# A two-layer hybrid attention block: one software pipeline per layer over the passes of all three branches

## What is computed

```
h = rmsnorm(x) * (1 + scale) + shift        # scale, shift, gate from silu(c) @ ada_w
mla:  q, k, v through low ranks (384, 256), part of q and k rotated; keys: 256 context + 512 image
swa:  8 query, 2 key heads; keys: 256 context + a band of 128 each side; a sink in the softmax
ax:   8 query, 2 key heads, q and k normalised per head and rotated; all 768 keys
y_b = (softmax(q k^T) v * silu(z_b)) @ w_o_b               for b in mla, swa, ax
x   = x + gate * ((sum_b sigmoid(g_b) * y_b) @ w_out)
```

## Time and profile before

| | |
|---|---|
| median of three runs | 2379.16 us |
| the profiled execution | 2383.12 us, span 2383.2 us |
| TensorE busy, weight loads | 1965.2 us (82%), 1676.0 us (70%) |
| VectorE, ScalarE, GpSimd busy | 1079.5 us (45%), 893.4 us (37%), 622.4 us (26%) |
| chain of work that ended last | TensorE 61%, VectorE 20%, ScalarE 8%, GpSimd 5%, issue 4%, DMA 2% |
| projections in that chain | L941, 48% |
| data moved | 125.90 MB, mean 53 GB/s |

### The profile page before, as it was taken

One profiled execution on the slowest core, in us unless ns is written; L12 is line 12 of the kernel. 1 busy time (PEld: TensorE's weight loads), 2 busy tenths in 40 slices (PEclk: granted clock), 3 DMA queues, 4 the chain that ended last, 5 costly groups with the idle time before them and its releaser, 6 DMA issues.

```text
span 2383.2 us, 27657 instructions
## 1 busy us (share of the span) xinstructions
PE 1965.2 (82%) x11005; PEld 1676.0 (70%) x11005; DVE 1079.5 (45%) x2189; ACT 893.4 (37%) x1631; POOL 622.4 (26%) x328
## 2 busy tenths in 40 slices
PE   4487777998888997787998967777997889676987
PEld 2376666888777885676887956666786778566767
DVE  0334667202566215787322343666224652568323
ACT  2323445312445213665322122444322442456332
POOL 5411110223100232222343231120342015220452
PEclk7597999999879997998998977898997799789999
DMA  5200000222000221122223110000231013200342
GB/s 191 69 24 19 18 18 1 53 71 71 18 5 10 53 76 47 42 62 54 75 84 125 47 63 24 14 23 14 80 98 36 5 28 102 62 14 1 84 133 98
DMA packets 183441, 125.90 MB, mean 53 GB/s; under 512 B 6478, under 2 KB 178064, under 8 KB 183312
## 3 DMA queue, kind: packets, MB, share of 16 engines
q1 hardware_dynamic: 177520, 108.57, 16.3%
q10 hardware_dynamic: 5792, 15.56, 1.9%
HBM read 119.91 MB, written 4.19 MB: 52 GB/s over the span
## 4 chain that ended last, share of the span: by engine, by line
PE 61%; DVE 20%; ACT 8%; POOL 5%; issue 4%; DMA 2%; ACTq 0%; DVEq 0%; SPq 0%
PE acc L941 48%; PE wide L964 4%; PE ptp L979 3%; DVE nmax L1477 3%; DVE pt_m L1495 2%; PE acc L999 2%; DVE e_m L1490 2%; POOL swapped L1308 2%; POOL rot L1311 2%; ACT pt_m L1202 2%; PE acc L1000 2%; DVE o_t L1502 1%; ACT e_m L1193 1%; DVE swapped L1381 1%; DVE rot L1382 1%
## 5 line engine op out<-in xcount | busy, mean ns | idle before, releaser
L1287 POOL TENSOR_TENSOR w_lo<-w_raw,w_hi 128x1024 fp32r<-128x1024 f32 (+3 forms) x236 | 494.9, 2109 | 1366.7 <-ACT w_hi L1126 1366.6
L941 PE MATMUL acc<-h_hi,w_hi 128*128 128x512 f32 (+2 forms) x1288 | 470.9, 366 | 27.6 <-POOL h_lo L1320 14.7
L941 PE MATMUL acc<-h_lo,w_hi 128*128 128x512 f32 (+2 forms) x1288 | 468.9, 364 | 0.0
L941 PE MATMUL acc<-h_hi,w_lo 128*128 128x512 f32 (+2 forms) x1288 | 468.3, 364 | 0.0
L941 PEld LDWEIGHTS acc<-h_hi,w_hi 128*128 128x128 f32 (+1 forms) x1288 | 252.0, 196 | 70.3 <-POOL h_lo L1320 15.5
L1126 ACT ACTIVATE w_hi<-w_raw 128x1024 fp32r<-128x1024 f32 (+3 forms) x236 | 216.4, 932 | 195.3 <-PE acc L941 146.1
L941 PEld LDWEIGHTS acc<-h_hi,w_lo 128*128 128x128 f32 (+1 forms) x1288 | 251.2, 195 | 36.6
L941 PEld LDWEIGHTS acc<-h_lo,w_hi 128*128 128x128 f32 (+1 forms) x1288 | 251.2, 195 | 35.9
L1477 DVE TENSOR_REDUCE nmax<-wide 128x1 f32<-128x768 f32 (+4 forms) x240 | 189.4, 789 | 22.1 <-PE wide L964 11.0
L1495 DVE TENSOR_TENSOR pt_m<-ptp,pt_m 128x512 fp32r<-128x512 f32 x208 | 142.4, 687 | 96.4 <-ACT pt_m L1202 95.1
L1160 ACT ACTIVATE th<-acc 128x512 f32<-128x512 f32 x108 | 56.9, 527 | 338.1 <-PE acc L941 336.9
(11 more groups left out here) (183 smaller groups left out, 3717.4 us busy)
## 6 DMA issues: line engine op xcount, KB each, us to landing
w_raw<-in_w_in SPq DMA_DIRECT2D x102, 512.0 KB, 3.9
w_raw<-in_ada_w SPq DMA_DIRECT2D x48, 512.0 KB, 3.5
w_raw<-in_w_out SPq DMA_DIRECT2D x16, 512.0 KB, 3.4
xres<-in_x ACTq DMA_DIRECT2D x2, 2048.0 KB, 10.9
w_raw<-in_w_o_mla SPq DMA_DIRECT2D x16, 256.0 KB, 2.8
w_raw<-in_w_o_swa SPq DMA_DIRECT2D x16, 256.0 KB, 2.9
w_raw<-in_w_o_ax SPq DMA_DIRECT2D x16, 256.0 KB, 2.8
w_raw<-in_mla_w_uq SPq DMA_DIRECT2D x8, 288.0 KB, 2.9
```

The source lines that it names most:

```text
L941: ins = nc.tensor.matmul(dst, lhs, rhs, start=first, stop=last)
L1287: nc.gpsimd.tensor_tensor(w_lo[:, c % SPLIT_SLOTS, 0:k], w_raw[:, c % RAW_SLOTS, 0:k], f(w_hi[:, c % SPLIT_SLOTS, 0:k]), ALU.subtract).the ...
```

## The change

`schedule()` is written anew. `attention()` is now called once per layer, over the passes of all three branches in one list. Around one pass `cur` it works off the tiles of the pass before, `old`, in a fixed pattern with five gaps; in a gap `fill` takes steps of a queue of projections in proportion to what is left to do. The queue holds the next heads' q, k and v, the keys and values of the next branch, the z tiles of the branch, and the g and y tiles of the branch before it (in the third branch those of the second). The g and y tiles of the third branch, and all `ada` columns of the layer (in layer 0 those of layer 1 too), stand behind the attention. Two z tiles and the ax key are projected before the attention begins.

Scores now have one PSUM area `wide` of three banks: a unit's scores come in two parts, `SA` and `SB`, and `SB` waits for the exponential of the unit before, whose bank it shares; the maximum follows `SB`. Values have a bank `pv` of their own, projections alternate between both `acc`. z is applied before the output is there: `E` of z writes into `o_t`, and `O` multiplies the output in, by a second operation of VectorE. The output of a branch is split after its last pass, by four operations on ScalarE and four on VectorE (`og`). The sink is no longer a score column: ScalarE takes its exponential and VectorE adds it to the sum. The cosine and sine tables are loaded by GpSimd's queue. Weights have four slots, three while attention runs, in which raw and low part share memory: a slot is free when the last matmul that reads it is done.

```diff
-RAW_SLOTS, SPLIT_SLOTS = 3, 4
+SLOTS, TIGHT = 4, 3
+E_UNITS = 4
+ROPE_LAG, COPY_LAG = 7000, 3500
...
+        c = len(chunks) - 1
+        slot = min(range(SLOTS if roomy[0] else TIGHT), key=lambda s: -1 if slot_last[s] is None else slot_last[s])
+        slot_of.append(slot)
+        slot_prev.append(slot_last[slot])
+        slot_pv.append(n["pt"] if slot >= TIGHT else 0)
+        slot_last[slot] = c
+        return c
...
-                        while n["split"] < (chunk_ids[0] if oldest is None else oldest) + SPLIT_SLOTS:
-                            c = n["split"]
-                            emit("W", c=c, reuse=chunk_last.get(c - SPLIT_SLOTS, 0))
+                        held = chunk_ids[0] if oldest is None else oldest
+                        ahead = chunk_ids[-1] + (SLOTS if roomy[0] else TIGHT) - 2
+                        while n["split"] <= ahead and (n["split"] <= chunk_ids[-1] or n["split"] - TIGHT < held):
+                            emit("W", c=n["split"])
...
+        def fill(left, branch):
+            rest = sum(c for _, c in steps) + sum(q["cost"] for q in queue if BRANCHES.index(q["of"]) <= BRANCHES.index(branch))
+            credit[0] += rest / max(left, 1)
+            while refill():
+                run, cost = steps[0]
+                if cost > 0 and credit[0] < cost / 2:
+                    return
+                credit[0] -= cost
+                steps.pop(0)
+                run()
+        def settled(groups):
...
+        def SA(u):
+            key = (u["branch"], u["h"])
+            while key not in ready or not settled(ready[key]):
+                forced()
+            while now[0] < max(g["at"] + (ROPE_LAG if g.get("roped") or g["kind"] == "kx" else COPY_LAG) for g in ready[key]) and refill():
+                forced()
+            if any(g.get("hl") and "low_n" not in g for g in ready[key]):
                 flush()
             u.update(n=n["s"], slot=n["s"] % E_UNITS, x=n["x"],
-                     ready_free=max(g["v"] for g in ready[u["h"]]), ready_l=max(g.get("low_n", 0) for g in ready[u["h"]]))
+                     ready_free=max(g["v"] for g in ready[key] if "v" in g), ready_l=max(g.get("low_n", 0) for g in ready[key]))
             n["s"] += 1
...
-            emit("S", u=u)
-        def M(u):
...
+            tick()
+        def SB(u):
+            if u["b"]:
+                emit("SB", u=u)
+                now[0] += sum(cost_of(nk, 3 if u["branch"] == "mla" else 2) for _, _, nk in u["b"])
+            emit("X", u=u)
             before = owner.get(u["slot"])
             u["e_free"] = before["pt_end"] if before else 0
             owner[u["slot"]] = u["pa"]
             emit("M", u=u)
-        def N(u):
-            emit("N", u=u)
-            u["pa"]["normed"] += 1
...
+        SA(ps[0]["units"][0])
+        for i in range(len(ps) + 1):
+            cur = ps[i] if i < len(ps) else None
+            old = ps[i - 1] if i else None
+            after = ps[i + 1] if i + 1 < len(ps) else None
+            tiles = list(old["tiles"]) if old else []
+            values = []
+            branch = (cur or old)["branch"]
+            def gap():
+                if cur:
+                    gaps[branch] -= 1
+                    fill(gaps[branch] + 1, branch)
+            def transpose():
+                if tiles:
+                    values.append(tiles.pop(0))
+                    T(values[-1])
+            def value():
+                if values:
+                    PV(values.pop(0))
+            if cur:
+                SB(cur["units"][0])
+            transpose()
+            gap()
+            if cur:
+                emit("N", u=cur["units"][0])
+                SA(cur["units"][1])
+            gap()
+            value()
+            transpose()
+            if cur:
+                SB(cur["units"][1])
+            gap()
+            value()
+            transpose()
+            gap()
+            if cur:
+                emit("N", u=cur["units"][1])
+            while tiles or values:
+                value()
+                transpose()
+            if old:
+                O(old)
+                if not cur or cur["branch"] != old["branch"]:
+                    while steps or any(q["of"] == old["branch"] for q in queue):
+                        forced()
+                    og(old["branch"], sums[0])
+            if after:
+                SA(after["units"][0])
+            gap()
+        while refill():
+            forced()
     def ada(l, j):
         slot = n["ada"] % 2
...
+        item((SWA, 0), "mla", tile_cost, lambda s: True, q_pair(SWA, 0))
+        item("values_s", "mla", 3 * cost_of(256, 48), lambda s: True, values_s)
+        z_item(1, 0)
+        for t in range(KO):
+            y_item(0, 2 * t)
+            if t + 1 < KO:
+                z_item(1, t + 1)
+                item((SWA, t + 1), SWA, tile_cost, lambda s, t=t: t == 0 or (SWA, 2 * t - 1) in s, q_pair(SWA, t + 1))
+                y_item(0, 2 * t + 1)
...
+        y_item(0, 2 * KO - 1)
+        z_item(2, 0)
+        for t in range(KO):
+            y_item(1, 2 * t)
+            if t + 1 < KO:
+                z_item(2, t + 1)
+                item((AX, t + 1), AX, tile_cost, lambda s, t=t: t == 0 or (AX, 2 * t - 1) in s, q_pair(AX, t + 1))
+            y_item(1, 2 * t + 1)
+        def to_og(branch, sums):
+            for t in range(KO):
+                g = high_low("og", t=t, l=l, o=sums, acc=n["acc"])()
+            og[branch] = g["low_n"]
+        attention(l, ready, ready_v, zs, queue, to_og)
...
+        emit("XL", l=l, tail=True, s=n["s"])
+        n["xl"] += 1
+        if l + 1 < LAYERS:
+            load_table("s")
+        for t in range(KD):
+            if t == 1 and l + 1 < LAYERS:
+                scale_table(l + 1, V_AXK)
+            ys = y_tile(l, 2, t, og)
+            roomy[0] = True
+            run_all(ys)
+            if t % 2 == 0:
+                run_all(ada(l, GATES[t // 2]))
+            if l + 1 < LAYERS:
+                run_all(ada(l + 1, t))
...
-        wide = [psum("wide0", 1024), psum("wide1", 1024)]
-        ptp = [psum("ptp0", 512), psum("ptp1", 512)]
+        pv, wide, ptp = psum("pv", 512), psum("wide", 1536), psum("ptp", 1024)
...
-                if c >= RAW_SLOTS:
-                    if new(w_lo_ready, c - RAW_SLOTS + 1):
-                        sp.wait_ge(w_lo_ready, c - RAW_SLOTS + 1)
+                if slot_prev[c] is not None:
+                    if new(acc_done, chunk_last[slot_prev[c]]):
+                        sp.wait_ge(acc_done, chunk_last[slot_prev[c]])
+                if new(pv_done, slot_pv[c]):
+                    sp.wait_ge(pv_done, slot_pv[c])
...
-                    sp.dma_start(dst, src).then_inc(raw_load[c % RAW_SLOTS], 16)
+                    sp.dma_start(dst, src).then_inc(raw_load[slot_of[c]], 16)
...
                     pa = e["pa"]
                     own, _ = o_rows(pa)
                     if new(o_copied, pa["o"] + 1):
                         dve.wait_ge(o_copied, pa["o"] + 1)
                     k = len(pa["units"]) * P
-                    nc.vector.tensor_tensor(o_t[own, pa["h"] // 2, o_tokens(pa)], acc[1][own, 0:k], o_half[own, 0:k], ALU.add).then_inc(o_free, 1)
+                    nc.vector.tensor_tensor(o_half[own, 0:k], pv[own, 0:k], o_half[own, 0:k], ALU.add).then_inc(o_sum, 1)
+                    if new(o_sum, pa["o"] + 1):
+                        dve.wait_ge(o_sum, pa["o"] + 1)
+                    if new(acc_free, pa["zs"]):
+                        dve.wait_ge(acc_free, pa["zs"])
+                    o = o_t[own, pa["h"] // 2, o_tokens(pa)]
+                    nc.vector.scalar_tensor_tensor(o, o_half[own, 0:k], 0.5, o, ALU.mult, ALU.mult).then_inc(o_free, 1)
                 elif ev == "MOD":
                     if new(acc_free, e["free"]):
```

720 lines of the change are left out of this document (369 added, 351 removed).

## The result

The changed kernel takes 2636.31 us (median of four runs, 2633.78 to 2638.7) against 2379.14 us before: a ratio of 1.106, interval 1.1031 to 1.1089. The forecast was 2289 us with a range up to 2410, so sign and size were both wrong. The profiled execution has a span of 2632.0 us. One number further down needs a word: of the four executions of the experiment barewarm one was disturbed (3732 us against 2496 to 2502), and its time and ratio go by the other three.

What follows compares the result with a forecast made beforehand. VectorE was taken to pace attention before, an in-order chain across engines after. Attention with its fill, 1510 us (1477 + 18 + 15), plus 783 for the rest gave 2293, predicted as 2289 us after the profiling offset; range 2150 to 2410.

Steps and rivals of the forecast that it cites:

- The chain of one pass: Attention image pass: program order ties VectorE, ScalarE and TensorE into one chain of 12.0 us, 12.5 with handoffs.
- The part outside attention: Start, first projections, tails, output, norms and end of both layers: 783 us in all.
- The rotation's own price: Rotated projections between attention parts: ScalarE waits 5.7 us for GpSimd, some 2 covered, leaving 3.7 us each.
- rival one: Attention: TensorE becomes the bound, its 1116 us stretch to 1213; total 2029 us, 2140 with rope waits; chance 0.18.
- VectorE sets the pace of the kernel before: Attention before the change: passes come every 6.4 us though TensorE needs 4.3, waiting for VectorE's output read.
- The projections put into the gaps are hidden under the chain as long as they fit: Attention gaps: projections cost nothing extra while they fit; a last-branch image pass in layer 1 has 10.7 us TensorE work.
- the price of an ordinary pass: Attention passes without rotations: 12.5 (latent), 11.2 (window), 13.4 us (axial) in layer 1; means 10.7, 9.9, 11.5 in layer 0.
- about 0.4 less for the maxima, 0.5 for the exponentials: Window branch image pass: shorter rows, also 0.7 less for the tile, 0.3 more for the sink, giving 11.2 us.
- GpSimd beside VectorE: Attention: GpSimd's weight splits beside every pass slow VectorE; 15 us added, bounds 0 and 120.
- the rival on the slower side: Attention: rotated projections hold ScalarE 7.9 instead of 3.7 us each, 126 us more, total 2415 us; chance 0.2.
- The range: Whole kernel: 2150 to 2410 us; the forecast's own 2210 to 2360 allows passes 1 us shorter or longer.

Runs made afterwards that it cites:

- barewarm: Changed kernel, projections in gaps cut to first and last matmul per group, twelve matmuls added before values of each tile but a pass's first; 2496.9 us, ratio 1.0483.
- cap: Changed kernel with the credit that gaps save up for projection steps bounded to twice what one gap is due; 2635.9 us, ratio 1.1059 to the kernel before.
- pipe: Changed kernel with the same work reordered within a pass, so that its loop is cut in three places; 2425.3 us, ratio 1.0172 to the kernel before.
- warm: Changed kernel with eight 256-column matmuls added before the values of every tile but a pass's first; 2632.2 us, ratio 1.1046 to the kernel before.

## Why the prediction was wrong

**What held.** The chain of one pass, step by step: it stands in the trace in the order that was walked through, and in the axial branch of layer 1, the one that was walked through in full, ordinary intervals take 13.6 us against the 13.4 priced. TensorE's matmuls in the gaps count little: leaving out a third of all gave 111 us. The part outside attention (783 against 804, with errors that partly cancel). The rotation's own price: 3.7 us each against 4.3 by leaving it out, with ScalarE waiting for it 28 times in attention for 4.4 us on average, as was said. TensorE did not become the bound (rival one), and no weight load (DMA) ends a wait of ScalarE in the attention stretches. That VectorE sets the pace of the kernel before was read from its rows; no run tested it. One reading was off without consequence: the trace has 11005 matmul records before and 10845 after, and the 160 between them are the sink's, not 80 of 10801.

**First failed step: "The projections put into the gaps are hidden under the chain as long as they fit".** The sum charged a pass for a mean step of 1.3 us on TensorE, for what a projection's read and weight split put in front of the chain, and for 3.7 us per rotation. In the 26 intervals with rotated projections that was 111 us above the price of a pass, and it measured 300. Of these 300 the runs place two parts: leaving the rotation out gives 128 back, and leaving out the matmuls takes these intervals down by 57. The rest, some 115 us if the two parts simply add, is neither. These projections also bring loads, weight splits and reads, which were kept in every run, so that they make up the rest is argued and not shown. Nor is it their coming in bunches: six gaps hold up to 128 projection matmuls and three rotations, but cap spread them and the time stayed.

**Second: the price of an ordinary pass.** 12.6 us against 11.3 as priced, 111 us over 88 intervals. It is not spread evenly. The 30 intervals of the window branch hold 63 of the 111 us: 11.5 us against 9.9 in layer 0 and 14.2 against 11.2 in layer 1. Its price was not walked through but taken from the axial one by four differences ("about 0.4 less for the maxima, 0.5 for the exponentials"), and this is the term that was sized worst.

GpSimd beside VectorE explains a part. The read of the output's PSUM half takes 0.42 us whatever GpSimd does. The second operation, which has two inputs in SBUF, takes 0.42 us in the 97 cases without a GpSimd operation beside it and 1.6 us in the 18 that lie beside one for more than half their time (changed kernel: ns min/median/max):

```profile
L1641 DVE TENSOR_TENSOR o_half<-pv,o_half x120: 401/422/430, 263.6 to 2472.6; 64x256 f32<-64x256 f32 x120
L1647 DVE SCALAR_TENSOR_TENSOR o_t<-o_half,o_t x120: 416/422/2179, 264.1 to 2473.1; 64x256 f32<-64x256 f32 x120
```

Summed over all of VectorE's operations, what lies over the lower quartile of the same line, names and form (counted where it is more than 15% over) is 102 us after and 39 before, and every operation counted overlaps one of GpSimd. That is 63 us more instead of the 15 taken, inside the stated bounds. In the ordinary intervals it is 58 us, so at most 0.65 us a pass; at most, because pipe has as much of it (62 us) in passes of 10.2 us. Adding matmuls to raise the clock left the ordinary interval at 12.6 us (warm). What remains, at least 0.6 us a pass, stays open.

**Third: intervals with a rotation.** This is a part of the first. The 20 under 25 us are 7.0 us above the price instead of 3.7, near the 7.9 of the rival on the slower side. But the rival's reason does not hold: leaving the rotation out gives 4.3 us each and not 7.9, and the kernel before pays just as much. The rival ended at 2415, still 220 short.

**The range.** It allowed a pass 1 us more or less. All the errors in attention lengthen, none shortens: the sum of steps had left out what came in addition, and 2 us in each of 120 passes are more than the whole gain of 90. The forecast gain of 3.8% was the difference of two numbers near 2300 us, one measured and one built from such a sum.

The Trainium skill (Perfetto Trace Analysis, Optimization Strategy) says that a kernel with several regimes, each with its own most-contended engine, may be improved by interleaving them. Here the regimes were interleaved, and the ratio is 1.106 in one order of the queues and 1.007 in the best other one that leaves the rotated read in its place. The sentence says "may", and these runs are a case in which it did not pay, since the loop that carries the latency lost as much as the dense work was worth.

## What to carry to other kernels

When work is interleaved over engines with queues in order, write down the loop of one pass with its crossings between engines first; it must be shorter than the work of the engine that is to be filled, or that engine goes on waiting. Cut it by placing an instruction that needs another engine behind work that does not (a high part ahead of an exponential, last values behind the next scores, a rotated read six events later). Mend the order first: it gave 211 us here, the place of the rotated read 94 to 103, and evening out the filler nothing in the slow order and 25 us in the better one. Price the filler with all that it brings (load, split, read, rotation) and not by its matmuls. And look at the list of instructions before the chip: the bunches of up to 17 steps stood in it.

## What was not expected of the hardware

Leaving 3726 of 10845 matmuls out lowered the granted clock from 0.87 to 0.66 and the time by 4% only. Adding matmuls that raised the clock from 0.78 to 0.90 in a stretch of 300 us changed it by 2 us. VectorE's operation with two inputs in SBUF took 1.6 instead of 0.42 us beside GpSimd, and the one on the same 64x256 elements with an input in PSUM did not change. The wait for GpSimd's rotation cost 128 and 129 us in two kernels with quite different orders, and moving one kind of read gave back 103 and 94 of it.
